# Gating and summing three branches head by head on GpSimd inside the delta stage, instead of by rows on VectorE in the closing

## The reference

```python
proj = rmsnorm(x, ln_mix_pre) @ w_in           # split into the inputs below
y_a = rmsnorm(o_a, hgrn_onorm) * silu(a_g)     # o_a: gated linear attention, 8 heads of 128
y_b = rmsnorm(o_b, gla_onorm) * silu(b_g)      # o_b: gated linear attention, 4 heads of 256
y_c = rmsnorm(o_c, gdn_onorm) * silu(c_g)      # o_c: gated delta rule, 8 heads of 128
g = sigmoid(merge).reshape(t, 3, D)
y = g[:, 0] * y_a + g[:, 1] * y_b + g[:, 2] * y_c
x = x + rmsnorm(y @ w_out, ln_mix_post)
x = x + rmsnorm(squared_relu_mlp(rmsnorm(x, ln_mlp_pre), w_up, w_down), ln_mlp_post)
```

## Time and profile before

| | |
|---|---|
| time, median of 3 runs | 4416.27 us (4415.55 to 4417.66) |
| profiled execution, own time | 4427.55 us |
| its span | 4425.8 us |
| TensorE busy | 4057.0 us (92%) |
| VectorE busy | 2735.1 us (62%) |
| ScalarE busy | 1845.4 us (42%) |
| GpSimd busy | 777.1 us (18%) |
| DMA, mean | 124 GB/s, 547.01 MB |

### The profile page before, as it was taken

How to read it: one execution, slowest core, us unless ns; L and a number is a source line. 1 busy time by engine, 2 the same in 40 slices (tenths; PEclk the granted TensorE clock), 3 DMA queues, 4 the chain that set the end, 5 groups by cost and what they waited for, 6 DMA issues and landing times. The chain is left out here.

```text
span 4425.8 us, 65769 instructions
## 1 busy us (share of the span) xinstructions
PE 4057.0 (92%) x25919; PEld 3160.6 (71%) x25919; DVE 2735.1 (62%) x3538; ACT 1845.4 (42%) x3370; POOL 777.1 (18%) x855
## 2 busy tenths in 40 slices
PE   8999889979997998999999999899779968999997
PEld 1788667758875776788788788666478844787786
DVE  1513677752167775556657777588656655656789
ACT  0412365542135553225633344466555523433533
POOL 0200400020040002000100220187423312222001
PEclk9999999989998998999999999899999989999998
DMA  7525421134232114134534444323231157224332
GB/s 261 175 105 168 140 70 46 51 126 151 103 129 99 51 44 146 67 128 146 196 116 171 160 157 176 117 92 107 97 118 64 40 205 266 81 105 157 110 124 81
DMA packets 274323, 547.01 MB, mean 124 GB/s; under 512 B 35961, under 2 KB 72153, under 8 KB 273773
## 3 DMA queue, kind: packets, MB, share of 16 engines
q1 hardware_dynamic: 274032, 543.05, 35.2%
HBM read 377.75 MB, written 165.23 MB: 123 GB/s over the span
## 5 line engine op out<-in xcount | busy, mean ns | idle before, releaser
L314 PE MATMUL p_ps<-p_wh,hi 128*128 128x512 f32 x896 | 352.7, 394 | 6.9 <-DVE p_wl L482 6.9
L1214 DVE TENSOR_TENSOR p_tl<-spare,p_th 128x1024 fp32r<-128x1024 f32 x156 | 196.9, 1263 | 250.9 <-ACT p_th L1032 250.9
L314 PE MATMUL p_ps<-p_wl,hi 128*128 128x512 f32 x896 | 350.7, 391 | 0.0
L314 PE MATMUL p_ps<-p_wh,lo 128*128 128x512 f32 x896 | 350.5, 391 | 0.0
L1032 ACT CAST p_th<-spare 128x1024 fp32r<-128x1024 f32 x156 | 163.6, 1049 | 420.6 <-PE p_ps L980 420.5
L980 PE MATMUL p_ps<-p_th,p_xh 128*128 128x512 f32 x784 | 306.5, 391 | 8.6 <-DVE p_tl L1214 8.6
L980 PE MATMUL p_ps<-p_th,p_xl 128*128 128x512 f32 x784 | 305.8, 390 | 0.0
L980 PE MATMUL p_ps<-p_tl,p_xh 128*128 128x512 f32 x784 | 305.7, 390 | 0.0
L980 PE MATMUL p_ps<-p_xh,p_th 128*128 128x512 f32 x672 | 265.3, 395 | 2.1 <-DVE p_tl L1214 2.1
L980 PE MATMUL p_ps<-p_xh,p_tl 128*128 128x512 f32 x672 | 264.0, 393 | 0.0
L980 PE MATMUL p_ps<-p_xl,p_th 128*128 128x512 f32 x672 | 263.7, 392 | 0.0
(11 more groups left out here) (493 smaller groups left out, 10479.0 us busy)
## 6 DMA issues: line engine op xcount, KB each, us to landing
spare<-w_in SPq DMA_DIRECT2D x56, 1024.0 KB, 5.8
p_raw<-w_in SPq DMA_DIRECT2D x40, 1024.0 KB, 5.8
pn_dram<-p_stg SPq DMA_DIRECT2D x128, 256.0 KB, 2.1
p_dram<-p_stg SPq DMA_DIRECT2D x112, 256.0 KB, 2.0
pt_dram<-p_stg SPq DMA_DIRECT2D x104, 256.0 KB, 2.4
m_w<-w_mod SPq DMA_DIRECT2D x12, 2048.0 KB, 12.9
zm_ogm<-pn_dram SPq DMA_DIRECT2D x48, 512.0 KB, 10.2
p_rows<-pt_dram SPq DMA_DIRECT2D x36, 512.0 KB, 3.7
```

The costliest lines, as they stand in the source:

```text
L314: mm = pe.matmul(ps[:, u, :], lhsT, rhs, start=(kk == 0 and q == 0), stop=(kk == KD - 1 and q == 2))
L1214: dve.tensor_tensor(tl[:, g % 2], (R11, T, R21, R12, R22, R11, R21)[i][:, 2 * u:2 * u + 2], th[:, g % 2], ALU.subtract).then_inc(s_lo, 1)
```

## The change

The gating and summing moves out of the closing into the delta stage, by heads of 128 columns for all 1024 rows, on GpSimd.

- Projections: in the three `merge` groups GpSimd adds 1.0 to each tile after tanh, 16 operations a group.
- Delta stage, SyncE: for each head eight loads of 1024 rows by 128 columns (three gates, three merge parts, the outputs of the two other branches), six in a first set and two in a second; `w_out` is loaded behind the last head's inputs instead of at the start, into the room of `conv` and `squares`.
- Delta stage, GpSimd: `factors(h)`, six operations of 128x1024, between `causal_decay` and `roots` in loops 1 to 7; `gather(h)`, two operations, behind `roots` in loops 2 to 8; `factors(7)` at the end of loop 7, before `output_roots(6)`. VectorE does the gather of the last head. A head is stored after its gather.
- Closing: `y` for all 8 tiles is loaded from `o_dram[2]`, and VectorE's merge is gone. The first blocks of `w_up` are loaded earlier (their room lies below the merge's now).

```diff
@@ seven_products, GpSimd
+                if isinstance(gain, float):
+                    for k in range(16):
+                        pool.wait_ge(s_act, n_act[q] + k + 1)
+                        x = stg[:, (PLAIN + k) % SG, :]
+                        pool.tensor_scalar(x, x, 1.0, None, ALU.add).then_inc(s_gn, 1)
@@ gated_delta
-        cv = sb("cv", [P, 2, 3, SEQ])
-        sq = sb("sq", [P, 2, NCK, CK])
+        cv, sq = C.conv, C.squares
+        TG, OA, GC = [C.gates[:, b] for b in range(4)], [C.gates[:, 4 + b] for b in range(2)], [C.gates[:, 6 + b] for b in range(2)]
@@ gated_delta, SyncE
             def stores(h):
-                sp.wait_ge(s["o_normed"], h + 1)
+                sp.wait_ge(s["gathered"], h + 1)
...
-            sp.dma_start(C.w_out[:], ins["w_out_2"][0].rearrange("(k p) n -> p k n", p=P)).then_inc(C.s_w_out, 16)
-            for h in range(H):
+            def columns(rows, c0):
+                return rows[:, c0:c0 + CK].rearrange("(c p) n -> p c n", p=P)
+
+            def first_factors(h):
+                c = h * CK
+                done = STEPS * (h - 1)
+                for b, (rows, c0), step in ((0, (C.pn_dram, N_AG + c), 4), (3, (C.pn_dram, N_BG + c), 3), (2, (C.o_dram[1], c), 5), (1, (C.pn_dram, N_M + c), 6)):
+                    if h > 0:
+                        sp.wait_ge(s["multiplied"], done + step)
+                    sp.dma_start(TG[b], columns(rows, c0)).then_inc(s_tg[b], 16)
+                if h > 1:
+                    sp.wait_ge(s["gathered"], h - 1)
+                sp.dma_start(OA[h % 2], columns(C.o_dram[0], c)).then_inc(s_oa[h % 2], 16)
+                sp.dma_start(GC[h % 2], columns(C.pn_dram, N_CG + c)).then_inc(s_gc[h % 2], 16)
+
+            def second_factors(h):
+                for b, j, step in ((0, 1, 1), (1, 2, 2)):
+                    sp.wait_ge(s["multiplied"], STEPS * h + step)
+                    sp.dma_start(TG[b], columns(C.pn_dram, N_M + j * D + h * CK)).then_inc(s_tg[b], 16)
+
+            first_factors(0)
+            for h in range(H + 1):
+                if h > 0:
+                    second_factors(h - 1)
                 if h + 2 < H:
                     load(h + 2)
...
                     load_rows(h + 2)
+                if h == H - 1:
+                    sp.wait_ge(s["tokens"], 3 * H)
+                    sp.wait_ge(s["sums"], H)
+                    sp.dma_start(C.w_out[:], ins["w_out_2"][0].rearrange("(k p) n -> p k n", p=P)).then_inc(C.s_w_out, 16)
+                if 0 < h < H:
+                    first_factors(h)
                 if h >= 2:
                     stores(h - 2)
@@ gated_delta, GpSimd
+            def factors(h):
+                a = OA[h % 2]
+                pool.wait_ge(s_oa[h % 2], 16 * (h // 2 + 1))
+                pool.wait_ge(s_tg[0], 16 * (2 * h + 1))
+                pool.tensor_tensor(a, a, TG[0], ALU.mult).then_inc(s["multiplied"], 1)
+                pool.drain()
+                pool.wait_ge(s_tg[1], 16 * (2 * h + 1))
+                pool.tensor_tensor(a, a, TG[1], ALU.mult).then_inc(s["multiplied"], 1)
+                pool.wait_ge(s_tg[2], 16 * (h + 1))
+                pool.wait_ge(s_tg[3], 16 * (h + 1))
+                pool.tensor_tensor(TG[2], TG[2], TG[3], ALU.mult).then_inc(s["multiplied"], 1)
+                pool.drain()
+                pool.wait_ge(s_tg[0], 16 * (2 * h + 2))
+                pool.tensor_tensor(TG[2], TG[2], TG[0], ALU.mult).then_inc(s["multiplied"], 1)
+                pool.drain()
+                pool.tensor_tensor(a, a, TG[2], ALU.add).then_inc(s["multiplied"], 1)
+                pool.wait_ge(s_gc[h % 2], 16 * (h // 2 + 1))
+                pool.wait_ge(s_tg[1], 16 * (2 * h + 2))
+                pool.tensor_tensor(GC[h % 2], GC[h % 2], TG[1], ALU.mult).then_inc(s["multiplied"], 1)
+
+            def gather(h):
+                pool.wait_ge(s["o_normed"], h + 1)
+                pool.drain()
+                pool.tensor_tensor(o[:, h % 2], o[:, h % 2], GC[h % 2], ALU.mult)
+                pool.drain()
+                pool.tensor_tensor(o[:, h % 2], o[:, h % 2], OA[h % 2], ALU.add).then_inc(s["gathered"], 1)
...
                 if h + 1 < H:
                     causal_decay(h + 1)
+                if 0 < h < H:
+                    factors(h - 1)
+                if h + 1 < H:
                     roots(h + 1)
+                if h >= 2:
+                    gather(h - 2)
+                if h == H - 1:
+                    factors(H - 1)
                 if h > 0:
                     output_roots(h - 1)
@@ gated_delta, VectorE, behind the loops
+            dve.wait_ge(s["o_normed"], H)
+            dve.wait_ge(s["multiplied"], STEPS * H)
+            last = o[:, (H - 1) % 2]
+            dve.tensor_tensor(last, last, GC[(H - 1) % 2], ALU.mult)
+            dve.drain()
+            dve.wait_ge(s["gathered"], H - 1)
+            dve.tensor_tensor(last, last, OA[(H - 1) % 2], ALU.add).then_inc(s["gathered"], 1)
@@ closing, SyncE
-                rows, b = slice(t * P, (t + 1) * P), t % 2
-                for j in range(NJ):
-                    sp.dma_start(g(b, j), C.pn_dram[rows, br[j]:br[j] + D]).then_inc(s_in[j][b], 16)
-                    sp.dma_start(mg(b, j), C.pn_dram[rows, N_M + j * D:N_M + (j + 1) * D]).then_inc(s_in[j][b], 16)
-                    sp.dma_start(o(b, j), C.o_dram[j][rows, :]).then_inc(s_in[j][b], 16)
+                sp.dma_start(y[:, t, :], C.o_dram[2][t * P:(t + 1) * P, :]).then_inc(s_y[t], 16)
...
+            for t in range(2, NT):
+                load(t)
             for t in range(NT):
-                if t + 2 < NT:
-                    sp.wait_ge(s_y, t + 1)
-                    load(t + 2)
-                if t == NT - 3:
-                    sp.wait_ge(s_y, NT - 1)
+                if t == 2:
                     for b in range(4):
                         load_block(0, b)
@@ closing, VectorE
-            merge(0)
-            merge(1)
             dve.wait_ge(s_post, 16)
             for t in range(NT):
-                if t + 2 < NT:
-                    merge(t + 2)
```

More of the change, by code:

```diff
@@ L1159, in _ @@
                 gain = groups[q]["gain"]
-                if gain is not None:
+                if isinstance(gain, float):
[3 more added lines that the diff above has]
+                        pool.tensor_scalar(x, x, 1.0, None, ALU.add).then_inc(s_gn, 1)
+                elif gain is not None:
                     n = gain.shape[-1]
@@ L2650, in gated_delta @@
         s_cv = [sem(f"convolved_loaded{b}") for b in range(2)]
+        s_tg = [sem(f"factor{b}_loaded") for b in range(4)]
+        s_oa = [sem(f"first_output_loaded{b}") for b in range(2)]
+        s_gc = [sem(f"third_gate_loaded{b}") for b in range(2)]
+        STEPS = 6
         block = st.enter_context(nc.Block())
@@ L2696, in _ @@
             load_rows(1)
-            sp.dma_start(C.w_out[:], ins["w_out_2"][0].rearrange("(k p) n -> p k n", p=P)).then_inc(C.s_w_out, 16)
-            for h in range(H):
+            def columns(rows, c0):
[19 more added lines that the diff above has]
+                    second_factors(h - 1)
                 if h + 2 < H:
                     load(h + 2)
-                if h + 2 < H:
                     load_rows(h + 2)
+                if h == H - 1:
[4 more added lines that the diff above has]
+                    first_factors(h)
                 if h >= 2:
                     stores(h - 2)
-            for h in range(H - 2, H):
-                stores(h)
+            stores(H - 1)
             for b in range(2):
@@ L3259, in closing @@
         s_post = sem("merge_gain_loaded")
-        s_in = [[sem(f"branch{j}_loaded{b}") for b in range(2)] for j in range(NJ)]
+        s_y = [sem(f"y_loaded{t}") for t in range(NT)]
         s_x = [sem(f"x_loaded{b}") for b in range(2)]
         s_xst = [sem(f"merged_rows_stored{b}") for b in range(2)]
-        s_y = sem("y_ready")
         s_T = sem("y_turned")
@@ L3452, in turn @@
                 for k in range(KD):
-                    mm = pe.transpose(pt[:, k, :], y[:, t % 2, k * P:(k + 1) * P], C.ident[:])
+                    mm = pe.transpose(pt[:, k, :], y[:, t, k * P:(k + 1) * P], C.ident[:])
                 mm.then_inc(s_T, 1)
@@ L3713, in _ @@
         def _(dve):
-            def merge(t):
-                b = t % 2
-                for j in range(NJ):
-                    dve.wait_ge(s_in[j][b], 48 * (t // 2 + 1))
-                    dve.scalar_tensor_tensor(g(b, j), mg(b, j), 1.0, g(b, j), ALU.add, ALU.mult)
-                    dve.drain()
-                    if j == 0:
-                        if t >= 2:
-                            dve.wait_ge(s_T, t - 1)
-                        dve.tensor_tensor(y[:, b], g(b, j), o(b, j), ALU.mult)
-                    else:
-                        dve.tensor_tensor(g(b, j), g(b, j), o(b, j), ALU.mult)
-                        dve.drain()
-                        e = dve.tensor_tensor(y[:, b], y[:, b], g(b, j), ALU.add)
```

(6 more changed lines are left out.)

24 lines of the change are left out of this document (11 added, 13 removed).

## The result

The changed kernel takes 4441.96 us (median of 4 runs, 4433.99 to 4445.1) against 4416.35 for the kernel before, measured beside it, 25.6 us more; the ratio of the paired runs is 1.0052, 95% interval 1.0040 to 1.0064, which makes +23 us (18 to 28). The forecast was 4456, its range 4420 to 4487; the time lies 14 us under the forecast, inside the range. The profiled execution took 4433.99 us (span 4432.2).

What follows compares the result with a forecast made beforehand. TensorE was taken as nearly always busy in the delta stage, where GpSimd wasn't the bound but the roots had only 1.95 us of slack. 53 + 16 + 4 - 33 = +40 us gave 4456 us, range 4420 to 4487.

Steps and rivals of the forecast that it cites:

- the heads' term: Delta stage: roots' wait, lost turn and clock cost 8.85 us per head, +53 us over six loops (19 to 81).
- The wait for the roots: Delta stage: six GpSimd factors ahead of the roots make VectorE stand 4.5 us per head (3.2 to 5.8).
- The sign that was named: Delta stage: if the forecast is right, VectorE's L2937 waits over 3 us for the roots.
- The turn: Delta stage: VectorE's second scaling waits for one GpSimd gather operation, +2.35 us per head (0 to 4.7).
- The clock: Delta stage: TensorE's clock falls after the new wait, costing 2.0 us per head (0 to 3.0).
- The end: Delta stage's end: GpSimd's chain of last gathers, factors and output roots delays the last store, +16 us (12 to 20).
- The projections: Three tanh groups get 16 GpSimd operations each, 2.4 us a group, nothing behind the last; +4 us (0 to 7).
- The closing: First transpose 13.5 us earlier, tiles without late y 19.2 us less; -33 us together (-37 to -25).
- The bare stall: Rival, delta stage: VectorE waits for its roots but loses neither turn nor clock; +12 us, 4428; chance 0.15.
- Cheaper operations: Rival, delta stage: factor operations cheaper than the rows show; at 1.6 us roots are in time, -13 us, 4403; chance 0.12.
- A slower order of landings: Rival, delta stage: GpSimd comes first both times and loads land in 8 to 10 us; +69, 4485; chance 0.13.
- the row chain: Rival, closing: squares, root and scaling pace the merge as now, only 13.5 us come back; +59, 4475; chance 0.06.

Runs made afterwards that it cites:

- e4: Changed kernel with only the end reordered: output roots of head 6 moved ahead of the factors of head 7; ratio 1.0042.
- e12: Changed kernel plus one wait: after the roots GpSimd waits for both of VectorE's scalings before it gathers; ratio 1.0008.
- e7: e5 with output roots of head 6 before the last factors, and VectorE doing the last factor product and gathers of heads 6 and 7; ratio 0.9970.
- e5: Changed kernel with three factors before the roots, three behind the gather, GpSimd waiting for VectorE's scalings, stores issued before the next factor loads; ratio 0.9989.

## Why the prediction was right, and where it was off

- **The mechanism held, and the heads' term was far too large.** The six factors push the roots behind VectorE's need; VectorE waits, then loses a turn, then TensorE's clock falls. With small operations all of it is gone; with three ahead of the roots the wait is; with the added wait the turn is. The clock was not changed by itself: it is read in the rows behind the two delays. The range was wide enough to hold a term that was 19 us too high.
- **The wait for the roots: 2.5 us, not 4.5.** Two sizes were off. The reload that the fourth factor needs was through in time (a reload wait of 1.3 was taken, none was seen; the floor was right), and the operations and gaps took 14.5 us, not 14.9. The 2.5 given as the upper end of that wait belongs to the median landing of 7.6 us, not to the 10.0 named, which would give 4.9. The sign that was named, a wait over 3 us, did not come: it was 2.3 to 2.6.
- **The turn: 4.52 - 2.36 = 2.2 us on VectorE, 2.35 forecast.** The run with the added wait prices it, clock included, at 3.0 us per head. The wait and the turn make 4.7 us on VectorE; TensorE's idle time rose by 4.0.
- **The clock: 2.6 us of TensorE's busy time per head, 2.0 forecast**, 12.9 us over five heads; 8.6 of these remain with the added wait, so most of it goes with the wait for the roots.
- **Five loops, not six.** Loop 1 has factors and roots but no gather, and its scalings come later: 45.5 us against 44.7. Heads in all +33.7 (32.9 and 0.8) where +53 stood. The term's per-head size was 8.85; measured 6.6. This is the largest miss: about 11 us by the size in five heads, 8 by the sixth.
- **The end: +13.8, forecast +16,** by the chain as written. What e4 adds: bringing the output roots forward frees only 2.4 us, since GpSimd's own line ends last.
- **The projections: +5.0, forecast +4, but in another place.** "Behind the last group there is nothing to delay" was wrong: 3.4 us of the 5.0 are there. The last eight tiles are stored behind GpSimd's last eight operations (11.7 us, at 2817.61), and the next stage begins behind those stores. In the groups it is 0.8 us each.
- **The closing: -33.3 from its first load to the first MLP product, forecast -33.** The tiles' period and the surviving last wait were right.
- **The sum.** Heads 33.7, end 13.8, projections 5.0, closing -33.3, and -1.0 in the rest (the stage's start and the gated stage) give +18; the ratio says +23, interval 18 to 28. The sum lies at the low edge. The profiled execution of before was 11 us above its kernel's median, that of the changed kernel 8 below; stages that no edit touches differ by 12 us between the two traces (the group at 2628.83 against 2640.66). So the remaining 5 us are not assigned to a place. The forecast's +40 lies 22 us above this sum: 19 in the heads, 2 in the end.
- **The rivals.** The bare stall comes nearest to e12, which takes the turn away but leaves part of the clock's loss, and comes to +4 us, where +12 was named. "Cheaper operations" was wrong at its root: they take 2.36 us. A slower order of landings was not seen in the heads, and the row chain does not pace the closing: its tiles stand 15.48 us apart.

## What to carry to other kernels

When work moves onto an engine that has time, look at which side of its next deadline the time lies: here 15 us of operations fitted into a head, but ahead of the roots there were only 9.9 us of waiting and 2 of slack. Splitting the block around the deadline gave back most of the loss, and then a shared load and store queue became the limit, three times over (store behind loads, loads behind a store, a reload behind 4 MB of weights), each seen only as a wait on another engine. After each fix read the new last wait before sizing the next. And before pricing a meeting of two engines in a new order, look whether their operations still overlap at all.

## What the runs showed that I had not expected

- VectorE's scalings and GpSimd's operations, all with two SBUF inputs, cost time in both places where they met: 3.0 us a head in the changed kernel, 3.9 us in loop 1 of the kernel without the wait, where the roots had come early. GpSimd's gather operations took 3.08 and 3.15 us instead of 2.36, ahead of a wait of 11 us. The Trainium skill (SBUF — State Buffer, Who interferes with whom) calls the ports that the two engines share an exclusive lock; that whoever issues first holds them for the whole instruction it says of VectorE's two-port modes, which it says `tensor_tensor` does not have. The trace agrees with such a lock here too: a pair of 1.2 us operations was stretched by 2.2 us, nearly one GpSimd operation.
- The same gather takes VectorE 1.23 us and GpSimd 2.35 us (e7's end against e5's).
- The extra loads cost the heads nothing by themselves: with the operations at one column, the heads' DMA share rises from 0.17 to 0.55 and a head takes 42.42 us as before.
- TensorE's waits of 2.27 and 2.98 us in one head lowered the mean granted clock of the five heads from 1.00 to 0.92; with only the wait for the roots left it was 0.96.
